# Wide weight projections: chunks of half the depth by 512 columns in place of the whole depth by 256

## The reference, cut to what matters

```
xn = rmsnorm(h); q, f, i, g = split(xn @ w_in)       # layer 0: 1024 x 4096
h = h + (rmsnorm(recurrence(q, f, i)) * silu(g)) @ w_out
k, v = split(rmsnorm(h) @ w_kv); q = rmsnorm(h) @ w_q  # layer 1: 1024 x 1536 each
h = h + attention(q, k, v) @ w_o
# PEER, after each mixer
q = rmsnorm(h) @ peer_w_q                            # 1024 x 2048
experts, gates = top 16 of the sums of two top 16 of q against sub_keys
h = h + sum_e gelu(x . u[e]) * gate[e] * v[e]
```

## Time and profile before

| what | value |
|---|---|
| median of 3 runs | 1640.22 us |
| the profiled execution | 1638.91 us, its span 1636.8 us |
| PE busy | 1134.2 us (69%), 5152 instructions |
| VectorE busy | 1122.1 us (69%), 2947 instructions |
| GpSimd busy | 1054.2 us (64%) |
| ScalarE busy | 272.6 us (17%), 806 instructions |
| data moved | 647.16 MB in 164245 packets, 395 GB/s over the span |
| mean granted TensorE clock | 0.848 |

### The profile page before, as it was taken

One profiled execution on the slowest core, in us unless ns is written; L12 is line 12 of the kernel. 1 busy time (PEld: TensorE's weight loads), 2 busy tenths in 40 slices (PEclk: granted clock), 3 DMA queues, 4 the chain that ended last, 5 costly groups with the idle time before them and its releaser, 6 DMA issues.

```text
span 1636.8 us, 16492 instructions
## 1 busy us (share of the span) xinstructions
PE 1134.2 (69%) x5152; PEld 688.3 (42%) x5152; DVE 1122.1 (69%) x2947; ACT 272.6 (17%) x806; POOL 1054.2 (64%) x1030
## 2 busy tenths in 40 slices
PE   7988777786787458865578667786668755545556
PEld 7976454354464135533335334343326521111122
DVE  2659887675675886965566688685657796767552
ACT  2222112121113101111111201111211311111110
POOL 0007776775765677667765677667776577777772
PEclk9999888898898788977799778997889977777778
DMA  9878999999999999999999999999999999999997
GB/s 353 318 320 302 379 387 410 411 412 410 412 411 412 409 407 406 412 411 409 409 413 412 410 389 400 413 412 409 410 411 411 357 411 409 410 409 409 409 409 304
DMA packets 164245, 647.16 MB, mean 395 GB/s; under 512 B 18624, under 2 KB 18880, under 8 KB 151616
## 3 DMA queue, kind: packets, MB, share of 16 engines
q0 software_dynamic: 147456, 536.94, 82.8%
q1 hardware_dynamic: 16704, 109.17, 16.5%
HBM read 644.99 MB, written 1.05 MB: 395 GB/s over the span
## 4 chain that ended last, share of the span: by engine, by line
DMA 38%; POOL 21%; issue 16%; DVE 12%; PE 11%; ACT 1%; POOLq 0%; DVEq 0%; ACTq 0%; PEldq 0%
DMA v_ring<-in_v,idx_all 18%; DMA u_ring<-in_u,idx_all 17%; POOL u_ring L451 10%; POOL v_ring L451 10%; PE acc L1536 8%; DVE u_ring L927 4%; DMA arena<-in_v,idx_all 3%; DVE w_ring L927 1%; DVE xn L509 1%; POOL arena L451 1%; PE bank L1294 1%; PE bank L1272 1%; DVE arena L509 1%; PE bank L1298 1%; POOL w_ring L451 1%
## 5 line engine op out<-in xcount | busy, mean ns | idle before, releaser
L1536 PE MATMUL acc<-v_ring,diag 128*64 128x512 f32 x1536 | 481.8, 705 | 258.4 <-ACT diag L1194 207.6
L451 POOL DMA_INDIRECT u_ring<-in_u,idx_all x448 | 456.8, 1020 | 276.7 <-issue 129.6
L451 POOL DMA_INDIRECT v_ring<-in_v,idx_all x448 | 473.5, 1057 | 237.0 <-PE acc L1536 137.4
L927 DVE SCALAR_TENSOR_TENSOR u_ring<-u_ring,xrep 128x1024 f32<-128x1024 f32 x384 | 463.1, 1226 | 208.2 <-DMA u_ring<-in_u,idx_all 197.0
L1536 PEld LDWEIGHTS acc<-v_ring,diag 128*64 128x64 f32 x1536 | 196.7, 159 | 522.5 <-issue 261.1
L1536 PE MATMUL acc<-arena,gains 128*64 128x512 f32 x256 | 85.2, 731 | 75.2 <-DMA arena<-in_v,idx_all 74.8
L1536 PE MATMUL acc<-v_ring,gains 128*64 128x512 f32 x256 | 85.2, 705 | 71.7 <-DMA v_ring<-in_v,idx_all 71.1
L1181 ACT ACTIVATE ez<-zi 128x8 f32<-128x8 f32 x64 | 13.4, 209 | 575.2 <-DVEq L937 572.5
L1298 PE MATMUL bank<-w_ring,xT 128*128 128x256 f32 x448 | 103.8, 393 | 4.9 <-ACTq L981 4.9
L1294 PEld LDWEIGHTS bank<-xT,w_ring 128*128 128x128 f32 x896 | 103.2, 196 | 6.6 <-issue 5.7
L1294 PE MATMUL bank<-xT,w_ring 128*128 128x128 f32 x896 | 104.8, 280 | 0.5 <-ACTq L981 0.5
(11 more groups left out here) (176 smaller groups left out, 1246.0 us busy)
## 6 DMA issues: line engine op xcount, KB each, us to landing
w_ring<-in_wall SPq DMA_DIRECT2D x86, 1024.0 KB, 8.5
u_ring<-in_u,idx_all POOLq DMA_INDIRECT x448, 16.7
v_ring<-in_v,idx_all POOLq DMA_INDIRECT x448, 16.8
u_ring<-in_wall SPq DMA_DIRECT2D x4, 1024.0 KB, 10.0
v_ring<-in_wall SPq DMA_DIRECT2D x3, 1024.0 KB, 9.3
arena<-in_wall SPq DMA_DIRECT2D x3, 1024.0 KB, 10.7
gains<-in_gains SPq DMA_DIRECT2D x5, 512.0 KB, 13.4
kept<-in_wall SPq DMA_DIRECT2D x2, 1024.0 KB, 12.5
```

The source lines that it names most:

```text
L451: nc.gpsimd.indirect_dma_start(out=ring[:, r, :], out_offset=None, in_=table, in_offset=bass.IndirectOffsetOnAxis(ap=idx_all[:, at:at + 1] ...
L927: V.scalar_tensor_tensor(out=ring[:, r, :], in0=ring[:, r, :], scalar=1.0, in1=token_rows(phase)[r % PACK], op0=ALU.mult, op1=ALU.mult, ac ...
L1536: ins = M(acc[half(r % PACK), s], diagonal((first + n) * RING + r)[0], ring[:, r, s], start=False, stop=last and q + PACK == RING)
```

## The change

The 48 chunks keep their size, their number and their order. A pair of neighbouring chunks is cut the other way: the first holds blocks 0 to 3 of the depth for all 512 columns, the second blocks 4 to 7. The layout in DRAM stays, so each load now reads, for each partition, 4 KB out of each of two chunk rows. Each matmul streams 512 columns as two runs of 256. The output projection of layer 0 uses two turns of the PSUM banks where it used three, its pieces become 512 and 512, and the second half of the transposed tokens is waited for before the second chunk.

```diff
-PIECES = (((0, 512, 2, 0), (512, 256, 1, 512), (768, 256, 1, 0)), ((0, 512, 1, 0), (512, 512, 1, 512)))
+PIECES = (((0, 512, 2, 0), (512, 512, 2, 512)), ((0, 512, 1, 0), (512, 512, 1, 512)))
...
+WIDE_FIRST, WIDE_END = W_IN + 8, W_O
...
             def load(n):
-                src = wall_d[CHUNKS[n]]
+                row = CHUNKS[n]
                 kind, at = HOMES[n]
+                if WIDE_FIRST <= row < WIDE_END:
+                    pair, s = row - row % 2, slice(row % 2 * CHUNK // 2, (row % 2 + 1) * CHUNK // 2)
+                    src = wall_d[pair:pair + 2, :, s].rearrange("c p m -> p c m")
+                    to = lambda a: a.rearrange("p (c m) -> p c m", c=2)
+                else:
+                    src = wall_d[row]
+                    to = lambda a: a
...
-                    sp.dma_start(w_ring[:, at % WRING, :], src).then_inc(w_in[at % WRING], 16)
+                    sp.dma_start(to(w_ring[:, at % WRING, :]), src).then_inc(w_in[at % WRING], 16)
...
             def project_chunk(out, c):
-                w = next_chunk().rearrange("p (k n) -> p k n", k=KT_D)
-                for k in range(KT_D):
-                    ins = M(out[:, c * 256:(c + 1) * 256], xT[:, k, :], w[:, k, :], start=k == 0, stop=k == KT_D - 1)
+                w = next_chunk().rearrange("p (c k n) -> p k c n", c=2, k=KT_D // 2)
+                for k in range(KT_D // 2):
+                    at = c * KT_D // 2 + k
+                    ins = M(out[:, :].rearrange("p (c n) -> p c n", c=2), xT[:, at, :], w[:, k, :, :], start=at == 0, stop=at == KT_D - 1)
                 ins.then_inc(w_used, 1)
...
+            def project_wide(turns):
+                pe.wait_ge(transposes_read, count.transposes)
+                for _ in range(turns):
+                    out = take_turn()
+                    for c in range(2):
+                        project_chunk(out, c)
...
                 out = take_turn()
-                w = next_chunk().rearrange("p (k n) -> p k n", k=KT_D)
-                for k in range(KT_D):
-                    if k % 4 == 0:
-                        pe.wait_ge(transposes_read, count.transposes - 1 + k // 4)
-                    ins = M(out[:, 0:256], xT[:, k, :], w[:, k, :], start=k == 0, stop=k == KT_D - 1)
-                ins.then_inc(w_used, 1)
-                project_chunk(out, 1)
-                for _ in range(2):
-                    project_chunk(take_turn(), 0)
+                for c in range(2):
+                    pe.wait_ge(transposes_read, count.transposes - 1 + c)
+                    project_chunk(out, c)
+                project_wide(1)
                 yield
```

More of the change, by code:

```diff
@@ L339, in by_slot, with run @@
             return a[:, 0:heads, :].rearrange("p n (q s) -> p n q s", s=PACK)
-        def run(rows_of, mixer, route, leads=False):
+        def run(rows_of, mixer, route):
             def side(phase):
@@ L353, in run @@
                 for done, kinds in enumerate(plan):
-                    if not leads:
-                        rows_of(phase, done, done + 1)
+                    rows_of(phase, done, done + 1)
                     for kind in kinds:
@@ L360, in run @@
                             parts[phase + 1] = next(following)
-                    if leads:
-                        rows_of(phase, done, done + 1)
                 if len(plan) < ROUNDS:
@@ L1057, in hgrn @@
                 count.chunks += 4
-                count.banks += 3
+                count.banks += 2
                 yield
@@ L1278, in lent_read, with project_across @@
                 pe.sem_inc(lent_free, 1)
-            def project(turns, across, by_half=False):
+            def project_wide(turns):
[4 more added lines that the diff above has]
+                        project_chunk(out, c)
+            def project_across(turns, by_half=False):
                 pe.wait_ge(transposes_read, count.transposes - (1 if by_half else 0))
@@ L1288, in project @@
                         w = next_chunk().rearrange("p (k n) -> p k n", k=KT_D)
-                        if across:
-                            for b in range(2):
-                                for k in range(KT_D):
[L1292 to L1296, removed]
+                        for b in range(2):
                             for k in range(KT_D):
-                                ins = M(out[:, c * 256:(c + 1) * 256], xT[:, k, :], w[:, k, :], start=k == 0,
-                                        stop=k == KT_D - 1)
+                                if by_half and k == KT_D // 2:
+                                    pe.wait_ge(transposes_read, count.transposes)
+                                ins = M(out[:, (2 * c + b) * P:(2 * c + b + 1) * P], w[:, k, b * P:(b + 1) * P],
+                                        xT[:, k, :], start=k == 0, stop=k == KT_D - 1)
                         ins.then_inc(w_used, 1)
@@ L1325, in hgrn @@
                     transpose_new(width(xn))
-                project(1, True, t == 0)
+                project_across(1, t == 0)
                 yield
-                project(2, True)
+                project_across(2)
                 yield
-                project(1, True)
-                project(1, False)
+                project_across(1)
+                project_wide(1)
                 yield
@@ L1400, in attention @@
                 transpose_new(width(xn))
-                project(1, False)
+                project_wide(1)
                 yield
-                project(2, False)
+                project_wide(2)
                 yield
                 transpose_new(width(xn))
-                project(1, False)
+                project_wide(1)
                 yield
-                project(2, False)
+                project_wide(2)
                 transpose_new([ks[:, n * HD:(n + 1) * HD] for n in range(NKH)])
```

## The result

The changed kernel takes 1644.61 us (median of 8 runs, 1643.68 to 1647.04) against 1640.62 us for the kernel before (8 runs, 1638.34 to 1642.85): ratio 1.0025, 95% interval 1.0016 to 1.0034, or 4.0 us more by the two medians (2.6 to 5.6 by the interval). Every ratio and interval leaves out executions that fell into a second, slower state of the chip.

What follows compares the result with a forecast made beforehand. The prediction held transfer time to bound nearly all the run, except the first 126 us of serial compute. Matmuls 0, seam +1.0 and packets +2.0 gave +3.0 on the 1640.2 median: 1643.2 us, range 1639 to 1647.

Steps and rivals of the forecast that it cites:

- TensorE, 0: 48 projection chunks as 4 matmuls by 512 columns: no time gained or lost; first side -0.7 to +0.4 us.
- The rival that had kept a part of it: TensorE's first-side chunks: fewer, longer matmuls save their fixed part, -1.4 us, total 1641.8; chance 0.06.
- The seam, +1.0: Layer 0, output projection to routing: wider last piece lengthens the serial chain by 1.0 us, bounds 0.6 and 1.3.
- first index wait: GpSimd's wait for the first indices at the start, forecast at 124.9 us in place of 123.9.
- The packets, +2.0, bounds 0 and 4.1: Weight loads under full DMA: 36 chunks in 4 KB packets cost 0.057 us each, 2.0 us together.
- the point of decision: Chunk price, 0.064 us, from which the rival of dearer packets on full engines (+5.1, 1645.3; chance 0.20) wins.
- Weights late: Rival on weight loads: smaller packets delay landing to 11 to 22 us, TensorE stands waiting, 1648.8; chance 0.05.
- the rival's turn-taking: Two DMA queues alternating packet by packet: half-size packets give weights 1/2 of turns, not 2/3; landing a third longer.
- Dips filled: Rival on three dips in transfer rate: shorter instruction queues fill half of 13 us lost, 1636.7; chance 0.08.

Runs made afterwards that it cites:

- e4: Changed kernel with 8 KB loads and the old three-piece seam, 512-column matmuls in 44 of 48 chunks; ratio 1.0001 against the kernel before.
- e3: Kernel before with only layer 0's output projection seam changed (pieces 512 and 512, one PSUM bank, still 256 columns); ratio 1.0004, +0.7 us.
- e1: Changed kernel with chunks laid out in DRAM so loads read 8 KB a partition again; ratio 1.0002 against the kernel before, +0.3 us.
- e8: Kernel before with all 98 chunks loaded as 2 KB packets, four pieces 64 bytes apart; ratio 1.0083, 13.6 us more.
- e2: Kernel before with only the loads of the 48 chunks split into 4 KB packets, compute unchanged; ratio 1.0018, +3.0 us.
- e11: Kernel before with weights laid out partition by partition and 30 pairs of chunks each loaded by one 2 MB DMA; ratio 1.0012, slower.
- e9: Kernel before with all 98 chunks loaded as 4 KB packets, two pieces 64 bytes apart; ratio 1.0030, 4.9 us more.
- e10: Kernel before with all 98 chunks loaded as 4 KB packets, two pieces 1 MB apart; ratio 1.0041, 6.7 us more.
- e12: Kernel before with weights laid out partition by partition in DRAM, every chunk still loaded by itself at 8 KB; ratio 1.0003.

## Why the prediction was right

1643.2 us was forecast, +3.0, with a chance of 0.42 for slower and 0.50 for no change, and a range of 1639 to 1647. 1644.6 us was measured, +4.0: inside the range, at the edge between the two likeliest outcomes. By its steps:

- **TensorE, 0.** Right: 7.03 us for two chunks against 7.07 in the 12 chunks of the first side, and e4 at 1.0001. The burst of `w_o` was the right row to read; the pace that the Trainium skill gives for streams in "TensorE: Matmul & The Clock Gate", section "Back-to-back issue gap" (wide ones cheaper by the column), does not show in these float32 streams. The rival that had kept a part of it (1.4 us for a fixed part of each row; its own figures, 96 rows of 0.014 us, give 1.3) found at most some 0.3 us: the single chunks begin 5.21 us apart where it was 5.24.
- **The seam, +1.0.** Right: 0.88 us in three profiles. e3 has +0.7 in time, with an interval that alone would not show it. The forecast for the first index wait, 124.9 for 123.9, came out at 124.8, and that was luck: in the changed kernel's profile one burst before the seam took 1.63 us longer (last section), and it began 0.84 us earlier. That phase 1 pays nothing is not shown: a second 0.9 would make 1.8, which e3's interval holds (to +2.1) and e1's ends at.
- **The packets, +2.0, bounds 0 and 4.1.** Right in kind and somewhat small: the forecast had 0.057 us a chunk, from two totals over 200 us that differ by 0.27 MB. That these two came so near was partly luck, since e3 with the same loads moved 81.87 MB in the second stretch; read from its profile, the same comparison gives nothing. e8, the firmest of the experiments, has 9.0 ns a packet, 8 x 9.0 = 0.072 us a chunk and 2.6 us for 36; e2 has 3.0, and the two stretches above give 0.07 a chunk. As far as the intervals tell, this is the term that moved the result from just inside 0.2% to just outside: the text had put the point of decision at 0.064. The skill's rule ("DMA: Bandwidth & Descriptors", section "Why small descriptors are slow (HBM only)") points the same way, and the estimate that the prediction worked out from it, 1.1 us for the 36 chunks, is less than half of the measured 2.6 to 3.0.
- **Weights late.** The landing did grow, 8.5 to 9.5 us in the median and 16.5 to 19.6 at worst, less than the third more that the rival's turn-taking asked for, and nothing waited; in e8 it came to 16.3 and 31.2 and still nothing waited behind the first side. e11 shows what it looks like when it is real.
- **Dips filled.** No. The three stretches of the earlier trace rows moved 13.77, 7.37 and 6.40 MB after, for 14.16, 7.05 and 6.26 before. The first moved 13.39 (e4) to 14.26 MB (e2) in kernels that differ in time the other way, so it tells nothing of the change.

What the prediction did not have is a reason why the profile of before was short: it alone of all has no fall of the clock at the place that the last section shows, worth more than a microsecond there. It had seen the 1.3 us between that execution and the median and moved its sum by them, and so it did not go wrong by it. Adding up the two profiles' 5.6 us as the change's price would have.

## What to carry to other kernels

Where the transfer engines are full for the whole run, count packets as well as bytes: the edit was made to TensorE, where it was worth nothing, and was paid in packets on a queue that no view calls a bottleneck. A suspected cost of 2 us in 1640 is only just seen when it stands alone (e2: 1.3 to 4.6 us), but it can be priced by multiplying it: four pieces on all chunks gave 13.6 us and the price of one packet to a sixth. A microsecond on a chain is read between two rows of one profile, not from when the chain ends in two profiles. When halves become one whole ahead of a serial chain, the last piece's length is the price, whatever the number of instructions saved.

## What the runs showed of the hardware

While the 16 engines were full, a packet on the weights' queue had a fixed part of 9 to 10 ns beside its bytes, between 2 KB and 8 KB (an estimate from e8, e9 and e2; 7.5 to 10.5 by the firmest, e8).

In the first side TensorE's granted clock fell in the profiles of all the other kernels and not in that of the kernel before. The stretch from 90 to 94 us, of the kernel before, the changed one and e2:

```profile
90.00:94.00 4.00, 2.71 (x20) 1.00 1.01 424
```

```profile
90.00:94.00 4.00, 4.00 (x23) 0.59 1.01 426
```

```profile
90.00:94.00 4.00, 3.33 (x18) 0.66 1.01 422
```

The columns are the stretch, its length, PE busy (instructions), the granted clock as a share of 2.4 GHz, and DMA. After idle times of 2.3 and 1.2 us, the same in all three, the clock stood at full level in the first and for a good part at half (1.2 GHz) in the others, and 16 matmuls took 2.05, 3.68 and 3.29 us. e1, e3, e4, e8, e9, e10, e11 and e12 show 0.64, 0.66, 0.60, 0.58, 0.50, 0.50, 0.60 and 0.50 there, whether their compute was changed or not; so it is a matter of the single execution as far as these profiles tell, and why it fell in one and not in another is not shown. It puts 1.2 to 1.6 us into this burst. The stream of 256 matmuls from 11 us on differs as well, 30.4 (e3) to 31.7 us (e12) with the same instructions. So the first index wait moves by more than the seam is worth: 125.0, 124.5, 126.1, 124.9 and 126.6 us in e2, e8, e9, e11 and e12, which all have the compute of the kernel before, and its 123.9.
